# A hybrid decoder block on one core: all loops written out, and the waits of the recurrence in a new order

## The reference, cut to what matters

```python
def gated_delta_rule_chunked(q, k, v, g, beta):          # 4 heads of 128, CHUNK tokens at a time
    ...
    A = jnp.where(strict, jnp.einsum('bhnid,bhnjd->bhnij', k_beta, k) * decay, 0.0)
    T = lax.linalg.triangular_solve(eye + A, eye, left_side=True, lower=True)
    ...
    def step(state, inp):
        v_new = u_n - w_n @ state
        o = qd_n @ state + a_n @ v_new
        state = state * jnp.exp(gl_n) + kd_n.T @ v_new
        return state, o

h = x
h = h + hybrid_mixer(rms_norm(h), w_in, ..., w_out)       # gated DeltaNet heads beside a short convolution
h = h + memory_cross_attention(rms_norm(h), rms_norm(mem), w_xq, w_xk, w_xv, w_xo)
h = h + (silu(rms_norm(h) @ w_gate) * (rms_norm(h) @ w_up)) @ w_down
out = rms_norm(h, norm_final_g)
```

## Time and profile before

| | us |
|---|---|
| device time, median of 3 runs | 2923.04 (2922.69 to 2924.07) |
| profiled execution: span from the first to the last instruction | 2921.6 |
| PE busy in the profiled execution | 2881.8 (99% of the span) |
| DVE, ACT, POOL busy | 1859.1, 1145.3, 1479.3 |
| DMA traffic | 372.41 MB, 127 GB/s in the mean |

### The profile page before, as it was taken

One profiled execution on the slowest core, in us unless ns is written; L12 is line 12 of the kernel. 1 busy time (PEld: TensorE's weight loads), 2 busy tenths in 40 slices (PEclk: granted clock), 3 DMA queues, 4 the chain that ended last, 5 costly groups with the idle time before them and its releaser, 6 DMA issues.

```text
span 2921.6 us, 43014 instructions
## 1 busy us (share of the span) xinstructions
PE 2881.8 (99%) x14070; PEld 2394.2 (82%) x14070; DVE 1859.1 (64%) x2636; ACT 1145.3 (39%) x2049; POOL 1479.3 (51%) x1214
## 2 busy tenths in 40 slices
PE   8999999999999999999999999999999999999998
PEld 8888788888888888887888878888888888888786
DVE  2565566655359777777877556665634866665778
ACT  5532545434234333334543254443423433333334
POOL 7422455452226555568972244445322655555886
PEclk9999999999999999999999999999999999999999
DMA  7522222151113444467643232224111222224764
GB/s 260 209 96 102 94 80 72 61 177 51 58 72 114 165 152 163 165 222 246 228 144 144 100 109 73 72 65 166 65 44 74 82 108 108 97 93 146 260 192 169
DMA packets 179210, 372.41 MB, mean 127 GB/s; under 512 B 17104, under 2 KB 58128, under 8 KB 179088
## 3 DMA queue, kind: packets, MB, share of 16 engines
q1 hardware_dynamic: 116592, 301.06, 29.6%
q10 hardware_dynamic: 62496, 69.78, 7.0%
HBM read 268.51 MB, written 102.27 MB: 127 GB/s over the span
## 4 chain that ended last, share of the span: by engine, by line
PE 93%; DVE 2%; DMA 1%; POOL 1%; issue 1%; ACT 1%; SPq 0%; DVEq 0%; ACTq 0%; POOLq 0%
PE PS L3018 21%; PE PS L3020 21%; PE PS L3019 21%; PE PS L1991 2%; PE PS L1995 2%; PE PS L1993 2%; PE PS L1964 2%; PE PS L1962 2%; PE PS L1963 2%; PE PS L1875 2%; PE PS L3056 2%; PE PS L3052 2%; PE PS L3054 2%; PE PS L1897 2%; PE PS L3034 1%
## 5 line engine op out<-in xcount | busy, mean ns | idle before, releaser
L3018 PE MATMUL PS<-act_hi,w_hi 128*128 128x512 f32 (+1 forms) x1080 | 424.9, 393 | 1.0 <-POOL w_lo L2327 0.7
L774 POOL TENSOR_TENSOR down_lo<-down_raw,down_hi 128x1024 fp32r<-128x1024 f32 (+1 forms) x196 | 390.8, 2029 | 49.5 <-ACT down_hi L1248 49.2
L3020 PE MATMUL PS<-act_hi,w_lo 128*128 128x512 f32 (+1 forms) x1080 | 403.1, 373 | 0.0
L3019 PE MATMUL PS<-act_lo,w_hi 128*128 128x512 f32 (+1 forms) x1080 | 402.0, 372 | 0.0
L2352 POOL TENSOR_TENSOR w_lo<-raw,w_hi 128x256 fp32r<-128x256 f32 (+1 forms) x144 | 209.4, 1477 | 357.0 <-ACT w_hi L2447 357.0
L740 POOL TENSOR_TENSOR part_lo<-sum_s,part_hi 128x512 fp32r<-128x512 f32 x176 | 235.3, 1344 | 226.8 <-ACT part_hi L1228 226.3
L1705 DVE TENSOR_TENSOR copied<-copied,PS 128x512 f32<-128x512 f32 x264 | 177.4, 686 | 230.9 <-PE PS L3020 221.6
L3018 PE MATMUL PS<-op_t_hi,part_hi 128*128 128x512 f32 x704 | 274.4, 390 | 0.3 <-issue 0.2
L3020 PE MATMUL PS<-op_t_hi,part_lo 128*128 128x512 f32 x704 | 273.9, 389 | 0.0
L3019 PE MATMUL PS<-op_t_lo,part_hi 128*128 128x512 f32 x704 | 273.9, 389 | 0.0
L1789 DVE TENSOR_TENSOR h<-h,PS 128x512 f32<-128x512 f32 x344 | 218.1, 678 | 62.3 <-PE PS L3020 43.6
(11 more groups left out here) (368 smaller groups left out, 6432.1 us busy)
## 6 DMA issues: line engine op xcount, KB each, us to landing
raw<-in_w_units SPq DMA_DIRECT2D x132, 512.0 KB, 3.9
a_d<-copied SPq DMA_DIRECT2D x154, 256.0 KB, 2.2
down_raw<-a_d SPq DMA_DIRECT2D x154, 256.0 KB, 3.6
gu_raw<-in_w_units SPq DMA_DIRECT2D x44, 512.0 KB, 4.7
down_raw<-t_d SPq DMA_DIRECT2D x88, 256.0 KB, 3.0
down_raw<-in_w_units SPq DMA_DIRECT2D x66, 256.0 KB, 3.0
qkvz_d<-stage ACTq DMA_DIRECT2D x64, 256.0 KB, 2.5
raw<-att_d SPq DMA_DIRECT2D x32, 512.0 KB, 3.2
```

What stands on the lines that cost most here:

```text
L774: last = pool.tensor_tensor(flat(lo[:, :, :])[:, cs], flat(down_raw[m % 4][:, :, :])[:, cs], flat(hi[:, :, :])[:, cs].bitcast(f32), ALU.su ...
L3018: nc.tensor.matmul(out_ap, whi, xhi, start=start, stop=False)
L3019: nc.tensor.matmul(out_ap, whi, xlo, start=False, stop=False)
L3020: return nc.tensor.matmul(out_ap, wlo, xhi, start=False, stop=stop)
```

## The change

All `Fori` loops become Python loops: the same work, with constants for the loop's variable. And in the recurrence the waits change places; two waits on PE are dropped (ym_ready at y for l above 1, t_ready at the transpose for l above 2), and am_ready of level l + 1 moves up to step x of level l. Cut to its core:

```diff
                 if step[0] == "y":                                   # ACT
+                    act.wait_ge(S["xy_full"], n * 6 + l - 1)
                     act.wait_ge(S["y_full"], n * 6 + l)
-                    act.wait_ge(S["xy_full"], n * 6 + l - 1)
...
         def even_columns(dve, n, l):
+            dve.wait_ge(S["xt_full"], n * 6 + l - 1)
             dve.wait_ge(S["x_ready"], n * LEVELS + l)
-            dve.wait_ge(S["xt_full"], n * 6 + l - 1)
...
                 if step[0] == "x":                                   # DVE
+                    dve.wait_ge(S["x_ready"], n * LEVELS + l)
                     dve.wait_ge(S["xy_full"], n * 6 + l)
-                    dve.wait_ge(S["x_ready"], n * LEVELS + l)
...
             if step == "gram":                                       # PE
-                pe.wait_ge(S["kqn_ready"], n * 2 + 2)
                 pe.wait_ge(S["vrest_ready"], n)
                 if first:
                     pe.wait_ge(S["egb_ready"], n + 1)
+                pe.wait_ge(S["kqn_ready"], n * 2 + 2)
...
             if step == "a1t":
+                pe.wait_ge(S["scln_ready"], R * 2 if par == 1 or first else R * 2 - 1)
                 pe.wait_ge(S["am0_ready"], n + 1)
-                pe.wait_ge(S["scln_ready"], R * 2 if par == 1 or first else R * 2 - 1)
...
             if step[0] == "y":
-                pe.wait_ge(S["x_ready"], n * LEVELS + l)
-                pe.wait_ge(S["am_ready"], n * 6 + l)
                 if l == 1:
                     pe.wait_ge(S["vb_ready"], n + 1)
-                else:
-                    pe.wait_ge(S["ym_ready"], n * 12 + 2 * (l - 1))
+                    pe.wait_ge(S["am_ready"], n * 6 + l)
+                pe.wait_ge(S["x_ready"], n * LEVELS + l)
...
-                pe.wait_ge(S["xe_ready"], n * 6 + l)
                 if l == 2:
                     pe.wait_ge(S["attn_ready"], n + 1)
-                elif l > 2:
-                    pe.wait_ge(S["t_ready"], n * 6 + l - 1)
+                pe.wait_ge(S["xe_ready"], n * 6 + l)
...
             if step[0] == "x":
+                if l == 1:
+                    pe.wait_ge(S["on_ready"], n)
+                if l < LEVELS - 1:
+                    pe.wait_ge(S["am_ready"], n * 6 + l + 1)
                 pe.wait_ge(S["ym_ready"], n * 12 + 2 * l)
                 pe.wait_ge(S["t_ready"], n * 6 + l)
-                if l == 1:
-                    pe.wait_ge(S["on_ready"], n)
...
-                chunk_pe(0, 0, 0, True, False)
-                with pe.Fori(0, 3) as j:
-                    chunk_pe(j * 2 + 1, 1, j, False, False)
-                    chunk_pe(j * 2 + 2, 0, j + 1, False, False)
-                chunk_pe(TT - 1, 1, 3, False, True)
+                for m in range(TT):
+                    chunk_pe(m, m % 2, m // 2, m == 0, m == TT - 1)
```

More of the change, by code:

```diff
@@ L2072, in _ @@
             for half in range(NHALF):
-                with sp.Fori(0, NH) as j:
+                for j in range(NH):
                     for u in range(4):
@@ L2078, in _ @@
                 load_gain(g_x, norm_no(half, 1, 0))
-                with sp.Fori(0, 4) as j:
+                for j in range(4):
                     for u in range(3):
@@ L2198, in _ @@
                         sp.wait_ge(S[f"h_in{k}"], h_loads(half, 4))
-                with sp.Fori(0, NPAIR - 1) as j:
+                for j in range(NPAIR - 1):
                     for s in range(2):
@@ L2370, in _ @@
             for half in range(NHALF):
-                with pool.Fori(0, NH) as j:
+                for j in range(NH):
                     for u in range(4):
@@ L2377, in _ @@
                 decays_pool(pool, half * TT, 0, 0)
[L2378 to L2382, removed]
+                for m in range(TT):
+                    chunk_pool(pool, half, m, m % 2, m // 2, m == TT - 1, split_lo)
                 for c in range(4):
@@ L2425, in _ @@
                     part_lo(pool, half, 0, 1, k)
-                with pool.Fori(0, NPAIR - 1) as j:
+                for j in range(NPAIR - 1):
                     for s in range(2):
@@ L2678, in qkvz_act @@
                                     silu_z(act, half, j, R, g)
-                with act.Fori(0, NH - 1) as j:
+                for j in range(NH - 1):
                     qkvz_act(j, False)
@@ L2691, in _ @@
                 load_z(act, half, 0, 0)
[L2692 to L2696, removed]
+                for m in range(TT):
+                    chunk_act(act, half, m, m % 2, m // 2, m == 0, m == TT - 1, split_hi)
                 end_act(act, half)
@@ L2751, in _ @@
                 gate_up_act(act, half, 0, 1, lambda k: part_hi(act, half, 1, 0, k))
-                with act.Fori(0, NPAIR - 2) as j:
+                for j in range(NPAIR - 2):
                     gate_up_act(act, half, j + 1, 0, lambda k: part_hi(act, half, j + 1, 1, k))
@@ L2876, in _ @@
                 dve.wait_ge(S["out_stored"], 16 * half * EARLY)
-                with dve.Fori(0, NH) as j:
+                for j in range(NH):
                     R = half * NH + j
@@ L2892, in _ @@
                 start_dve(dve, half)
[L2893 to L2897, removed]
+                for m in range(TT):
+                    chunk_dve(dve, half, m, m % 2, m // 2, m == 0, m == TT - 1)
                 def first_add(t):
@@ L2983, in _ @@
                 gate_up_dve(dve, half, 1, 0, lambda: weight_sums(dve, half, 1, 1))
-                with dve.Fori(0, NPAIR - 2) as j:
+                for j in range(NPAIR - 2):
                     gate_up_dve(dve, half, j + 1, 1, lambda: weight_sums(dve, half, j + 2, 0))
@@ L3358, in qkvz_pe @@
                             last.then_inc(S[f"qkvz_full{b}"], 1)
-                with pe.Fori(0, NH - 1) as j:
+                for j in range(NH - 1):
                     qkvz_pe(j, False)
@@ L3444, in _ @@
                 gate_up_pe(half, 0, 1, 2)
-                with pe.Fori(0, NPAIR - 1) as j:
+                for j in range(NPAIR - 1):
                     for s in range(2):
```

## The result

| | before | after |
|---|---|---|
| device time, median | 2922.86 (2920.41 to 2925.81) | 2929.56 (2928.74 to 2932.97) |
| ratio | | 1.0024, 95% interval 1.0016 to 1.0032 |
| profiled execution: span | 2921.6 | 2927.4 |

What follows compares the result with a forecast made beforehand. PE was taken as the bound, busy 2881.8 of 2921.6 us; -9.6 us from writing out the recurrence and +5.8 from the new waits gave -3.8, 2919.2 us, range 2911.5 to 2926.

Steps and rivals of the forecast that it cites:

- Projection and gate-up: nothing: Input projection, gate-up, SP's and POOL's loops: writing out gains nothing, as PE stays fully busy and others wait for it.
- Level entries and line 1917: Recurrence, 12 looped chunks: writing out gains 0.15 us at three counted levels, 5.4 us, and 1.1 us at vnew's product.
- State update: Transposes of v, chunks 2 to 7: 0.66 falls to written-out chunk 0's 0.44 without four DVE register operations; 3.1 us gained.
- New order of waits: the price: Recurrence: a late wait moved into a separate instruction costs 0.06 us, bounds 0.02 and 0.10; together +5.8 us.
- New order of waits: the place: DVE's Xm 0.06 us later at levels 2 to 5 of 16 chunks and level 6 of two: 4.0 us.
- Late waits riding on the operations: Rival, recurrence: late waits stay on the operations, leaving only the writing-out gain; -10.6 us, 2912.4 us, chance 0.29.
- PE running into the next late result: Rival, recurrence levels 4 and 5: the next late result takes back 3.6 us of gain; 2923 us, chance 0.14.
- Instruction fetch: Rival, mostly gate-up: about 45 more packets at 1.3 us each, deciding from 8 exposed; ten give 2932 us, chance 0.08.
- Sum: Whole kernel: -9.6 us from writing out and +5.8 from the new waits make -3.8, giving 2919.2 us.
- holes: Rival, after gate-up: PE's 3.97 us idle for h's reload and DVE's add may move 3 us either way; chance 0.05.
- The profile's own signs: Recurrence: line 1875 at 0.58 to 0.60, v's transposes 0.44, o's near 0.7, middle chunks 0.4 to 0.5 us shorter.
- wrong altogether: Sign in the profile after that would refute the forecast: a difference that lies outside the recurrence.

Runs made afterwards that it cites:

- late first: All loops written out, the waits the change drops dropped, PE's late wait written first, ACT and DVE as before the change; 2920.07 us, ratio 0.9985.
- DVE's old: The changed kernel with only DVE's two pairs of waits put back in the old order; 2922.76 us, ratio 0.9995.
- SP looped: The changed kernel with SP's three loops kept as loops; 2929.84 us, ratio 1.0021.
- POOL waits: The changed kernel with one wait added: at y4 POOL waits for DVE's copy Xe of level 5; 2949.76 us, ratio 1.0087.

## Why the prediction was wrong

By its own steps:

- **Projection and gate-up: nothing.** Right for PE's stream: 160.00 of 160.00 and 360.00 of 360.00 us. Wrong in the conclusion, for the heading also took in SP's loops, which I put down as "waiting for PE in the end". What they do sooner, two loads into the moment when ACT issues five, was never asked: 0.7 to 0.8 us in each chunk 0. Nor did taking the 26 branches of these two loops out of PE's queue give anything back: with everything outside the recurrence written out the kernel took 2926.93 us against 2924.01, no faster at least.
- **Level entries and line 1917.** Right: -0.16 at each of levels 2 to 5, one of them given back at line 1817, and -0.09 at line 1917; 0.57 a chunk with old waits against 0.54 predicted from these terms.
- **State update, 3.1 us.** Mis-sized: next to nothing came (0.66 still stands behind chunks 2, 4 and 6 with everything written out and old waits, and 0.62 to 0.63 behind 1, 3 and 5). The same view as the earlier trace rows there, the timeline of DVE, and POOL's operation under way:

```profile
419.47 0.66 PE PS L1858 x4
```

```profile
417.76 0.63 DVE L1581 TENSOR_SCALAR ost_t<-ost_ss 128x4 f32<-128x4 f32 x1
418.30 1.11 DVE L1587 SCALAR_TENSOR_TENSOR state<-state,gate_elast,PS 128x128 f32<-128x128 f32 x4
...
417.09 1.27 POOL L695 TENSOR_TENSOR am<-dec,first_mask 128x512 f32<-128x512 f32 x1
```

  What stands ahead of the four state operations is a tiny one, line 1581, and the four register operations went by while it ran. It takes 0.63 us here and 0.17 where POOL has nothing under way; under POOL it ends 0.02 to 0.03 us after POOL's operation, as it did in the kernel before. Chunk 0 was no control: the same tiny operation stands there too (348.29, 0.26 us in the kernel before), but PE has a slice of the projection between the product that raises kv_full and the next chunk, and reaches the transposes of v at 350.66, 1.1 us after the last state operation. The changed kernel has 0.44 only at that same place.
- **New order of waits: the price.** Right: DVE's separate wait costs 0.03 + 0.02 + 0.04 in the chain above, 0.05 to 0.06 at a level entry more than where the operation carries it. Even chunks lose 0.31 by it (mean -0.24 against -0.55), 0.30 predicted.
- **New order of waits: the place.** This is the step that failed. I priced the shift as 66 x 0.06 and took everything behind it to shift with it. At level 5 of odd chunks and of chunk 7 the copy slides behind the start of a POOL operation that it had just missed (0.08 us ahead of it with the old waits, 0.07 behind it with the new ones in most chunks), waits for that one to end, and takes 0.7 to 0.8 instead of 0.3: another 0.25 to 0.39 at y5 and 0.06 behind it. Odd chunks lose 0.8, chunks 7 lose 0.9. Together, the new waits cost (4.7 + 5.3) 10.0 us where I had 5.8.
- **Rivals.** Late waits riding on the operations: false for the changed kernel, and true where the loops are kept, a case that I did not work out. PE running into the next late result: right in kind, it ran into DVE's copy at level 5, but through POOL. Instruction fetch: I asked for eight exposed packets, most of them in gate-up, and found none there; one may be exposed elsewhere. Ahead of half 1's chunk 0 the loads of q and k are issued at 1699.43 and 1699.91 us. The DMA view of 1701.5 to 1704 after, and its waits ahead of and in chunk 0:

```profile
q8 instruction: 1, 0.02, 2.5%
...
ACT rn L901 <- DMA qk<-qkvz_d: 2.9, 1, 2.9
...
PE PS L1808 <- POOL sq_lo L682: 1.0, 1, 1.0
```

  The packet, 2.5% of 16 engines over 2.5 us or 1.0 us, falls between packets of those loads. ACT starts on them 5.57 us after the first issue, where it had been 3.98, and by way of POOL's low half PE's sum of norms comes late by 1.2 us. In four further kernels with the recurrence and more written out (late first; DVE's old; SP looped; POOL waits) the packet starts 2.6 to 3.1 us after the issue, and they lose 1.2 to 1.4 there. In the two with PE's and ACT's old waits it starts 3.9 us ahead of it, and they lose 0.0. In the other seven kernels no packet of 16 KB starts in the first 3.8 us of these loads; ACT starts on them after 3.9 to 4.3 us, and nothing is lost. All agree; none moved the packet alone, so it is a correlation with a mechanism, not a proof.
- **Sum.** Writing out -6.8 (12 x 0.57), new waits +10.0, SP's loads +1.4 and the stretch with the packet +1.2 make +5.8, which is the profiled execution's +5.9; the runs say +6.7. Start and holes, which vary by as much between two executions of one kernel, happen to cancel, and that is luck. The profile's own signs came out by halves: 0.60 at line 1872, 0.66 at the transposes of o and DVE's separate wait were as foretold, but the transposes of v stayed at 0.66, odd chunks are longer, and 1.2 us lie outside the recurrence, which I had called "wrong altogether". The range left out this outcome because each part was costed on its own, and the two halves of the change were added: alone they give -4.6 and -3.6 us, together +6.7.

## What to carry to other kernels

When a loop is written out, look again at which wait rides on the operation: with constants it was the one written first, so the late one goes first; in a loop a register operation took the wait written ahead of it, and the late one was better written last. After any shift of a few hundredths of a microsecond, look at which POOL operation is under way where the shifted DVE operation now starts, and not only at what waits for it. Here the loops on the critical path were worth writing out, and the covered ones were not: they gave nothing back, and they moved DMAs, and it may be instruction packets, into the way of other loads.

## What the runs showed that I had not expected

- A DVE copy of 128x256 float32 takes 0.29 us alone. One that starts under a POOL operation ends 0.15 us after that operation, however long that takes (up to 0.83 us at level 5), so a shift across the start of a POOL operation costs half a microsecond at once, and a shift within one costs nothing. DVE's subtraction with an operand in PSUM, line 1522, takes 0.42 in every one of 96 cases of a trace, under a POOL operation (30 in the kernel before) or not.
- ACT's issue of gcb<-gc_d takes 0.35 to 0.58 us, and 1.11 to 1.37 as the fifth of five issues wherever SP's loops are written out (0.94 once with SP looped).
- Size does not protect an operation from this: the DVE operation on 128x4 elements at line 1581 takes 0.17 us alone and up to 0.63 under POOL's.
